# Down projection in one 4 MB transfer, dealt operand, queue order by pieces, spread overflow list and a GpSimd norm half in a single-core decoder layer

## What is computed

```python
h = h + ssd_mixer(rms_norm(h, mixer_norm[0]), ...)                 # Mamba-2 mixer
h = h + memory_cross_attention(rms_norm(h, xattn_norm[0]), ...)    # 4 heads into mem
h = h + moe_ffn(rms_norm(h, ffn_norm[0]), ...)                     # top 4 of 32 experts
return rms_norm(h, final_norm)

def expert_block(xb, e):
    gu = xb @ w_gate_up[e] + b_gate_up[e]                          # (., 2048)
    gate = jnp.minimum(gu[..., :D_FF], SWIGLU_LIMIT)
    up = jnp.clip(gu[..., D_FF:], -SWIGLU_LIMIT, SWIGLU_LIMIT)
    act = (up + 1.0) * (gate * jax.nn.sigmoid(gate * SWIGLU_ALPHA))
    return act @ w_down[e] + b_down[e]
```

## Time and profile before

| | |
|---|---|
| median of three runs | 1248.57 us |
| the profiled execution | 1247.7 us |
| its span, first to last instruction | 1245.9 us |
| mean granted TensorE clock | 0.993 |
| TensorE busy | 1175.0 us (94%) |
| DMA moved | 454.30 MB, mean 365 GB/s |
| chain that ended last | TensorE 53%, DMA 42%, VectorE 3% |

### The profile page before, as it was taken

How to read it: one execution, slowest core, us unless ns; L and a number is a source line. 1 busy time by engine, 2 the same in 40 slices (tenths; PEclk the granted TensorE clock), 3 DMA queues, 4 the chain that set the end, 5 groups by cost and what they waited for, 6 DMA issues and landing times.

```text
span 1245.9 us, 15217 instructions
## 1 busy us (share of the span) xinstructions
PE 1175.0 (94%) x6198; PEld 621.5 (50%) x6198; DVE 391.1 (31%) x703; ACT 275.9 (22%) x421; POOL 7.5 (1%) x27
## 2 busy tenths in 40 slices
PE   9999999999999999998988999899999998999996
PEld 8998887898634433333333333334433333343432
DVE  5987677546312211111111112102211111112112
ACT  5655566345211101011000011001101011011102
POOL 1000000000000000000000000000000000000000
PEclk9999999999999999999999999989999999999999
DMA  9454333469799999999999999999999999999996
GB/s 340 155 203 142 129 135 136 162 262 378 304 407 413 434 426 429 431 431 430 433 433 430 429 436 426 433 417 430 436 426 430 429 431 430 432 423 428 432 424 249
DMA packets 49191, 454.30 MB, mean 365 GB/s; under 512 B 5692, under 2 KB 5860, under 8 KB 30084
## 3 DMA queue, kind: packets, MB, share of 16 engines
q1 hardware_dynamic: 48976, 453.73, 87.7%
q10 hardware_dynamic: 180, 0.07, 0.0%
HBM read 452.74 MB, written 1.05 MB: 364 GB/s over the span
## 4 chain that ended last, share of the span: by engine, by line
PE 53%; DMA 42%; DVE 3%; issue 1%; DVEq 1%; SPq 1%; ACT 0%
DMA ring<-in_moe_w_down 41%; PE ps L985 14%; PE ps L1013 11%; PE ps L647 3%; PE ps L649 3%; PE ps L648 3%; PE ps L1023 2%; PE ps L960 2%; PE ps L662 1%; PE ps L664 1%; PE ps L663 1%; PE ps L779 1%; DMA wring<-in_ssd_w_in 1%; DVE wlo L1504 1%; PE ps L1000 1%
## 5 line engine op out<-in xcount | busy, mean ns | idle before, releaser
L1013 PE MATMUL ps<-ring,wring 128*64 128x512 f32 x960 | 216.5, 597 | 49.3 <-DMA ring<-in_moe_w_down 49.3
L985 PE MATMUL ps<-odd_ring,wring 128*64 128x512 f32 x1024 | 225.5, 598 | 0.9 <-DVE wring L1871 0.8
L985 PE MATMUL ps<-ring,wring 128*64 128x512 f32 x1024 | 223.5, 594 | 0.0
L1136 ACT ACTIVATE wring<-ps 128x512 f32<-128x512 f32 (+2 forms) x101 | 52.4, 535 | 499.8 <-PE ps L985 424.4
L1013 PEld LDWEIGHTS ps<-ring,wring 128*64 128x64 f32 x960 | 65.1, 137 | 188.7 <-issue 112.5
L1863 DVE COPY wring<-ps 128x512 f32<-128x512 f32 x32 | 22.1, 691 | 404.7 <-PE ps L985 404.7
L985 PEld LDWEIGHTS ps<-odd_ring,wring 128*64 128x64 f32 x1024 | 73.7, 138 | 141.6 <-issue 139.6
L985 PEld LDWEIGHTS ps<-ring,wring 128*64 128x64 f32 x1024 | 71.9, 137 | 139.3 <-issue 139.1
L1871 DVE TENSOR_TENSOR wring<-ps,bguT 128x512 f32<-128x512 f32 x64 | 41.2, 685 | 296.7 <-PE ps L1000 296.7
L1136 ACT ACTIVATE ysb<-ps 128x512 f32<-128x512 f32 x36 | 21.4, 596 | 260.6 <-PE ps L1013 246.4
L960 PEld LDWEIGHTS ps<-wring 128*128 128x128 f32 x480 | 55.8, 191 | 23.5 <-issue 23.5
(11 more groups left out here) (312 smaller groups left out, 1311.6 us busy)
## 6 DMA issues: line engine op xcount, KB each, us to landing
ring<-in_moe_w_down SPq DMA_DIRECT2D x59, 2048.0 KB, 25.3
ring<-in_moe_w_gate_up SPq DMA_DIRECT2D x28, 4096.0 KB, 22.9
odd_ring<-in_moe_w_gate_up SPq DMA_DIRECT2D x26, 4096.0 KB, 24.7
wring<-in_ssd_w_in SPq DMA_DIRECT2D x9, 2048.0 KB, 8.5
odd_ring<-in_moe_w_gate_up SPq DMA_DIRECT2D x9, 2048.0 KB, 15.7
ring<-in_moe_w_down SPq DMA_DIRECT2D x10, 1024.0 KB, 33.8
wring<-in_xa_w_kv SPq DMA_DIRECT2D x4, 2048.0 KB, 8.0
wring<-in_ssd_w_out SPq DMA_DIRECT2D x4, 2048.0 KB, 7.9
```

The lines of the kernel that those rows point to most:

```text
L985: last = mm(ps[a][SLOTS * half:SLOTS * (half + 1), :], xs[:, m, c % 2, :], w[:, kk, c0:c0 + 512], start=s + kk == 0, stop=s + kk == GP)
L1013: last = mm(ps[D_BANK][SLOTS * half:SLOTS * (half + 1), :], act[:, k, :], w[:, kk, 512 * half:512 * (half + 1)], start=k == 0, stop=k == K ...
L1136: return nc.scalar.activation(out_, in_, func, **kw)
```

## The change

- `w_down` is read as row 8*p + k in partition p: one run of 32 KB for each partition. In the stream, down of an expert is one 4 MB transfer (`load_down_whole`) into both slots, issued when both halves of the down before it are used, and TensorE waits for all of it before the first matmul of `down`. Expert 0 and the last two experts keep their smaller transfers.
- To match, the moving operand of every `gate_up` matmul is 128 runs of 4 floats with a step of 8 floats, and the biases of gate and up are loaded as 64 rows of 1024 floats and turned by 8 transposes of 64x128 in place of 4 of 128x128.
- SyncE's loop is written out. Experts 3, 4, 25, 28 and 31 come in pieces (before: 3 and 31). `AHEAD` tells how many pieces of expert c+2 stand before down of c: 4 up to c = 22, then 3, 2, 2, 1, and 0 from c = 27.
- The overflow list and the down biases are no stop between two experts: their parts stand between the parts of expert 18 in `regular(..., lists=True)`. Some pairs of TensorE's loop are written out for that and for the piece counts.
- The second half of `xn` is scaled by GpSimd: a `tensor_tensor` with the gains (dealt by 4), a drain, and a `tensor_scalar` with the reciprocal that VectorE makes. VectorE's L1488 for that half and its drain are gone.

```diff
+BY_PIECES = (3, 4, 25, 28, 31)
+AHEAD = ((0, 4), (23, 3), (24, 2), (26, 1), (27, 0))
...
-        dn_dram = w_down.rearrange("e (s p k) n -> e s p k n", p=P, k=4)
+        dn_rows = w_down.rearrange("e (p k) n -> e p k n", k=KD)
+
+        def dn_dram(e, k0, k1):
+            return dn_rows[e, :, k0:k1, :]
...
+        def load_down_whole(sp, e):
+            whole = part(ring, GP * WP, (GP + DP) * WP).rearrange("p (k n) -> p k n", k=KD)
+            sp.dma_start(whole, dn_dram(e, 0, KD)).then_inc(d_ready[0], 16)
...
-                for s in range(DP):
-                    sp.wait_ge(dn_used, 2 * DP * i + (DP * (c - 1) + s + 1))
-                    load_down(sp, e, s)
-
-            reload_pieces(3)
-            reload_down(1, 0, 1)
-            reload_gate_up(4, 0, 4)
-            reload_down(2, 0, 2)
-            with sp.Fori(1, PAIRS - 4, 1) as i:
-                for c in (1, 2):
-                    reload_gate_up(2 * i + (c + 2), i, c + 2)
-                    reload_down(2 * i + c, i, c)
-            reload_gate_up(NE - 5, 0, NE - 5, range(0, GJ // 2))
-            reload_down(NE - 7, 0, NE - 7)
-            reload_gate_up(NE - 5, 0, NE - 5, range(GJ // 2, GJ))
-            for e in range(NE - 6, NE - 3):
-                reload_down(e, 0, e)
-                reload_gate_up(e + 2, 0, e + 2)
-            reload_down(NE - 3, 0, NE - 3)
-            reload_pieces(NE - 1)
+                sp.wait_ge(dn_used, 2 * DP * i + DP * c)
+                load_down_whole(sp, e)
+
+            for c in range(1, NE - 2):
+                e = c + 2
+                ahead = [n for first, n in AHEAD if c >= first][-1]
+                for part_, s0, s1 in ((0, 0, ahead), (1, ahead, GP)):
+                    if part_:
+                        reload_down(c, 0, c)
+                    if e in BY_PIECES:
+                        reload_pieces(e, range(s0, s1))
+                    else:
+                        reload_gate_up(e, 0, e, range(s0 // GS, s1 // GS))
...
+            pool.wait_ge(ld_g, 16)
+            pool.wait_ge(std, 2 * 3 + TC)
+            nc.gpsimd.tensor_tensor(xn[:, 1, :].rearrange("q (k p) -> q k p", k=GR),
+                                    h[:, 1, :].rearrange("q (p k) -> q k p", k=GR),
+                                    g_ffn.rearrange("q (p k) -> q k p", k=GR), ALU.mult)
+            pool.drain()
+            pool.wait_ge(rst_ok, 1)
+            nc.gpsimd.tensor_scalar(xn[:, 1, :], xn[:, 1, :], rst[:, 3, 1:2], None, ALU.mult).then_inc(normed, 1)
...
-                                c0 = 1024 * a + 512 * half
-                                last = mm(ps[a][SLOTS * half:SLOTS * (half + 1), :], xs[:, m, c % 2, :],
-                                          w[:, kk, c0:c0 + 512], start=s + kk == 0, stop=s + kk == GP)
+                                dealt = w[:, kk, 1024 * a:1024 * (a + 1)].rearrange("p (q h j) -> p h q j", h=2, j=4)
+                                last = mm(ps[a][SLOTS * half:SLOTS * (half + 1), :].rearrange("p (q j) -> p q j", j=4),
+                                          xs[:, m, c % 2, :], dealt[:, half, :, :], start=s + kk == 0, stop=s + kk == GP)
...
+                scatter_transpose(i, c)
+                if lists:
+                    turn_gate()
+                pe.wait_ge(gate_b, 2 * i + c)
+                pe.wait_ge(up_b, 2 * i + c)
+                gate_up(i, c, expert)
+                if lists:
+                    biases_and_counts()
+                if gathers:
+                    gather_half(i, 1, 0)
+                down(i, c - 1)
+                if lists:
+                    places()
+                transposes(i, c)
+                scatter(i, c - 1)
+                if lists:
+                    overflow_list()
...
             v.tensor_tensor(mask[:, :, :], rest, lg[:, :, :], ALU.not_equal).then_inc(mask_ok, 1)
-            norm_apply(3, 1, xn, h, g_ffn)
-            dve.drain()
             dve.wait_ge(rank_ps, 1)
```

More of the change, by code:

```diff
@@ L138, in build @@
         rows_b = part(ring, 20608, 20736)
-        bg_rows = part(ring, 10240, 10752)
+        bg_rows = part(ring, 11264, 12288)
         xn0 = part(ring, 4096, 6144, r="p (t n) -> p t n", t=TC)
@@ L169, in build @@
         wdt = part(wdt_f, 0, KD * HEADS, r="p (k h) -> p k h", k=KD)
+        gateT = part(wdt_f, 0, SEQ)
         lrow = nc.alloc_sbuf_tensor_at("lrow", [P, TC, P], F32R, offset=wdt_at)
@@ L253, in build @@
         wq_ok = sem("wq_ok")
+        rst_ok = sem("rst_ok")
         sums_ok, extra_ps = sem("sums_ok"), sem("extra_ps")
@@ L386, in load_down_rows, with transfers, g_loads @@
             rows = slice(2 * half, 2 * half + 2)
-            sp.dma_start(dn_w(s)[:, rows, :], dn_dram[e, s, :, rows, :]).then_inc(d_ready[s], 16)
+            sp.dma_start(dn_w(s)[:, rows, :], dn_dram(e, 4 * s + 2 * half, 4 * s + 2 * half + 2)).then_inc(d_ready[s], 16)
         def load_gate_up_group(sp, e, odd, j):
             sp.dma_start(gu_group(odd, j), gu_rows[e, j, :, :, :]).then_inc(g_ready[GP * odd + GS * j], 16)
-        def g_loads(n, c):
-            extra = (0 if n == GP + 1 else 1) if n >= GP else 0 if c < 2 else 1 if n else 2
-            if n % GS == 0:
-                return c // 2 + 1 + extra
-            return min(c // 2, 1) + 1 + extra + (1 if n >= GP and c >= NE - 1 else 0)
+        def transfers(n, e):
+            if e % 2 != n // GP:
+                return 0
+            if e == 1:
+                return 1 if n == GP + 1 else 2
+            if e == 2:
+                return 2 if n else 3
+            return 1 if e == 0 or e in BY_PIECES or n % GS == 0 else 0
+        def g_loads(n, e):
+            return sum(transfers(n, x) for x in range(e + 1))
         def d_loads(s, c):
-            return (c + 1 if c < NE else c - 1) + (1 if s == 0 else 0)
+            return 1 if s else (c + 1 if c < NE else c - 1) + 1
         block = ctx.enter_context(nc.Block())
@@ L1061, in last_experts, with turn_gate, biases_and_counts @@
                 scatter(i, 1, scatT_last).then_inc(fin_ps, 1)
-            def regular(i, c, expert, gathers=True):
-                scatter_transpose(i, c)
-                pe.wait_ge(gate_b, 2 * i + c)
-                pe.wait_ge(up_b, 2 * i + c)
-                gate_up(i, c, expert)
-                if gathers:
-                    gather_half(i, 1, 0)
-                down(i, c - 1)
-                transposes(i, c)
-                scatter(i, c - 1)
-                if gathers:
-                    gather_half(i, 1, 1)
-            def biases_and_list():
+            def turn_gate():
                 pe.wait_ge(gate_ok, 1)
+                pe.wait_ge(xsb_ok, MIDDLE + 2)
                 for t in range(TC):
-                    last = tr(ps[D_BANK][0:NE, P * t:P * (t + 1)], gate[:, t, :], ident)
+                    last = tr(ps[G_BANK][0:NE, P * t:P * (t + 1)], gate[:, t, :], ident)
                 last.then_inc(gT_ps, 1)
+            def biases_and_counts():
                 pe.wait_ge(gT_ok, 1)
@@ L1897, in _, with regular @@
             swiglu(0, 0, 0)
-            def regular(i, c, gathers=True, out=act):
+            def regular(i, c, gathers=True, out=act, lists=False):
                 if gathers:
```

103 lines of the change are left out of this document (62 added, 41 removed).

## The result

The changed kernel takes 1251.93 us (median of 8 runs, 1250.59 to 1252.86), the kernel before on the same chip 1246.37 (8 runs, 1244.95 to 1249.79): a ratio of 1.0043 (95% interval 1.0035 to 1.0052), **slower by 0.43%**. The forecast was 0.33% faster. The profiled execution of the changed kernel took 1252.24 us, with a span of 1250.4; clock 0.981 in place of 0.993.

A forecast was written before the change was run, and what follows sets the result against it. The DMA queue was taken to bound the stream, TensorE having 3.2 us to spare per expert. Terms sum to -4.1 us from 1247.7, giving 1243.6, plus 0.9 for the median: 1244.5 us, 0.33% faster; range 1240.5 to 1249.

The forecast's parts named there:

- A: Down in one transfer: 23 fewer transfers at 0.08 us, -1.8 us; its other side, TensorE's later start on down, priced 0.
- B: Dealt operand of the gate and up matmuls: runs of four floats cost nothing, 13.88 us an expert stays.
- C: Second norm half on GpSimd at the router: first gather earlier, -0.6 us, bounds -1.05 to +1.5.
- Rival 4: At the router GpSimd and VectorE hold each other up: norm term +1.5 us, total 1246.6; chance 0.06.
- D: First reloads, expert 4 in pieces: the thin queue behind down 1 fills, -0.7 us, bounds 0 to -0.9.
- E: Overflow list spread inside one expert instead of a stop: -0.4 us, bounds 0 to -0.45.
- F: Order of transfers at the end: 1.2 us of queue gaps partly closed, -0.6 us, bounds 0 to -1.2.
- G: Gate and up biases at 25 us: 8 transposes in place of 4, between 0 and +0.4 us, taken as 0.
- base: Starting time of the forecast: the one profiled execution's 1247.7 us, with the median 0.9 above.
- Rival 1: No measurable difference: the 0.08 us belong to the bytes and queue gaps only move; -1.65 us, 1246.9; chance 0.22.
- Rival 2: Gate and up matmuls, all 32 experts: the dealt operand makes TensorE the bound, up to 1365 us; chance 0.08.
- Rival 3: The whole down's later start becomes the bound: +0.5 us an expert in 25, 1257 us; chance 0.06.

The follow-up runs named there:

- e8: e5 with every down in two halves again: 1248.05 us, ratio 1.0021 to the kernel before.
- e11: The changed kernel with the negation of the router's two maxima moved from VectorE to ScalarE: 1251.57 us, ratio 1.0038.
- e4: e3 with the queue's order and pieces as in the kernel before, downs still whole: 1254.76 us.
- e3: The changed kernel with the norm half back on VectorE and biases loaded on 128 partitions (wrong places): 1248.41 us, ratio 1.0017.
- e5: The changed kernel with the norm half back on VectorE and the 64-partition bias load issued behind mem: 1245.63 us, ratio 1.0004.
- e9: e5 with the overflow list and down biases again as a stop between experts 16 and 17: 1246.89 us, ratio 1.0010.
- e10: The kernel before with only the gate and up biases loaded as 64 rows and turned by 8 transposes: 1248.05 us, ratio 1.0013.
- e1: The changed kernel with the second norm half back on VectorE: 1248.48 us, ratio 1.0020.
- e2: The changed kernel with the biases loaded on 128 partitions as before (wrong places): 1250.24 us, ratio 1.0045.

## Why the prediction was wrong, by its own steps

**A** right: 29.14, and 1.9 to 2.4 by e8 for 1.8. Its "other side" was priced at 0 for the steady part, rightly, but not for the two places where TensorE leads again, the list and the end.

**B** right: 13.96 us. By the rule that the prediction quotes of the Trainium skill (SBUF — State Buffer, "Door 1: The DMA port swizzle"), that a run of four float32 is free, the trace agrees. The choice was right, but one reason for it wasn't: 13.88 us for eight times 2048 floats of a partition is 1.7 us for 2048, beside VectorE's 1.2 for 1024, no pace far below VectorE's. The stepped weight load of the earlier trace rows and VectorE's operation of the earlier trace rows were the wrong neighbours, since both take single floats.

**C** is the largest error: -0.6 forecast, +3.5 measured, outside the bounds of -1.05 to +1.5. Two terms failed. Durations: the one-input pass took 2.85, its bounds were 1.0 to 1.9; the stepped two-input pass 3.9 with its hand-over, close to my poor end. Mechanism: I let the engines hold each other only over the two norm halves. GpSimd's first pass, once it has waited for VectorE's half, holds the next tensor_scalar (changed kernel) or tensor_tensor (e11) on VectorE until its own end, and these stand on the chain to the mask. Rival 4 named this (0.06 and +1.5); its price lacked this second hold (1.3 of 3.8) and the length of GpSimd's two passes in a row (2.45).

**D** not resolved, -0.7 forecast. The thin place is filled: 386 to 392 us moves 437 GB/s in place of 372. But from down 0 to down 3 the one kernel with whole downs and the old order (e4) takes 81.64 us, and twelve with the new order take 80.72 to 82.33 (e3 81.19, e5 81.84). With halves e8 has 82.08 to the last half of down 3, the kernel before 82.04.

**E** wrong in sign: +0.85 for -0.4 (four profiles with the spread list lose 1.1 on the mean, two of the kernel before 0.2). The work added within one expert isn't made up. Whether the stop would be better beside A stays open: e9's median says no better than the same.

**F** wrong: -0.6 forecast. From the moment when all of down 22 is there to the end, eleven profiles with whole downs and the new order take 239.4 to 240.9 us (mean 240.0), the two of the kernel before and e10's 239.1 to 240.0 (mean 239.5): +0.4 on the mean, +1.1 in e5 against the second profile of before. The 1.2 us of gaps were real, but the queue wasn't the bound there: TensorE was, and it waits 2.6 us for the whole down 29 and has its clock down for it (changed kernel, timeline):
```profile
1196.99 8.68 PE L1036 MATMUL ps<-ring,wring 128*64 128x512 f32 x32 [2.62 <-DMA ring<-in_moe_w_down]
```
**G** wrong: 0 to +0.4 forecast for the 8 transposes, +3.5 at the start in the changed kernel's profile, and 2.3 (e10), 2.9 (e1 to e5), 1.7 (changed kernel to e2) and 0.1 (e1 to e3) in medians. I costed the transposes and put the load itself, a DMA of another shape in the queue of the weights, at nothing without a reason.

The **base** was off the other way: 1248.6, where 35 runs give 1245.7. The miss of 7.4 us is then C 4.1, G 1.7 to 3.5, E 1.2, F 1.0 to 1.7 and D 0 to 0.7, less 2.2 to 2.9 of base: 5.1 to 9.0. The 7.4 lies inside, and the runs don't fix it more closely. The range was also cut short by a wrong sum: its own poor ends give 1248.6 + 1.5 + 1 = 1251.1, 1251.5 with G's 0.4, where it says 1249. The measured 1251.93 lies outside both. Rival 1 (moved gaps) is what e5 shows, with both faults out, for another reason than its own: the 0.08 us are a transfer's, but the end is TensorE's. Rival 2 didn't happen. Rival 3's mechanism was there at two places only, the list and down 29, not in each expert.

## What to carry to other kernels

Price every DMA that changes its shape, a small one too, by the piece that the chain waits for in the same queue. Before work goes to GpSimd, list what VectorE has to do beside it: here a tensor_scalar of two numbers a partition and a tensor_tensor stood still until GpSimd's two-input pass had ended. And ask of each gain in the queue whether the queue is still the bound where the kernel ends, and take a base from more than one profile.

## What the hardware did that I had not expected

- A 256 KB load as 64 rows of 4 KB, on 64 partitions, took the queues from 384 to 243 GB/s (e10: 169) at the same busy share, and a 2 MB transfer issued ahead of it landed 1.5 us later on the mean (six profiles, mean 19.55, against five, 18.08).
- VectorE's tensor_scalar of 128x2 took 2.88 us, and its tensor_tensor of 128x64 2.24, until GpSimd's two-input pass ended; memset, max and match_replace beside the same pass were not slowed. Beside GpSimd's one-input pass two tensor_tensor operations took 0.43 and 0.23 us, as without it.
- GpSimd needs 2.85 us for a contiguous one-input pass of 128x1024 float32, more than the 1.90 of the earlier trace rows for the two-input one there; a step of 4 adds 1.7 us to its two-input pass.
- A wait of TensorE of 1.49 us near 52 us left the clock at its upper level (2.4 GHz) in e11; one of 1.85 (changed kernel) is followed by a mean of 0.56 and 0.87 over the next 6 us. In the two profiles of the changed kernel 22 downs start behind 2.6 to 3.2 idle us: 18 of them take 8.5 to 10.0 us and 4 take 7.09. The 14 downs behind 1.5 idle us or less all take 7.09. In the stream this is hidden, at its end it isn't.
